# Decoder step with 64 experts: three experts at fixed places, second-layer weights in row pairs

## What is computed

```
x += MoE(RMSNorm(x))     # 64 sigmoid-routed experts, top 8 of 64 (in 4 of 8 groups), and 1 shared expert
expert e:  h = silu(xg @ w1[e]) * (xg @ w3[e]) * gate      # w1, w3: 1024 x 256
           y = h @ w2[e]                                    # w2: 256 x 1024
```

## Time and profile before

| | |
|---|---|
| time, median of 3 runs | 1083.21 us (1082.49 to 1084.88) |
| the profiled execution | 1083.57 us, span 1081.8 us |
| mean granted TensorE clock | 0.996 |
| PE busy | 1042.0 us, 96% of the span |
| DMA | 296.59 MB; 403 to 409 GB/s in most slices of the expert loop |
| DMA packets | 87203, of which 68453 under 8 KB |
| expert loop on TensorE | 365.2 us to 983.6 us |

### The profile page before, as it was taken

One profiled execution on the slowest core, in us unless ns is written; L12 is line 12 of the kernel. 1 busy time (PEld: TensorE's weight loads), 2 busy tenths in 40 slices (PEclk: granted clock), 3 DMA queues, 4 the chain that ended last, 5 costly groups with the idle time before them and its releaser, 6 DMA issues.

```text
span 1081.8 us, 11992 instructions
## 1 busy us (share of the span) xinstructions
PE 1042.0 (96%) x3692; PEld 513.9 (48%) x3692; DVE 454.0 (42%) x1286; ACT 166.4 (15%) x407; POOL 391.2 (36%) x459
## 2 busy tenths in 40 slices
PE   6999999899998999999999999999999989999996
PEld 4777555555544444444444444443444434443442
DVE  4200222345377634344343443443433343342884
ACT  3110023310120111111111111111110110112332
POOL 6000321200034544444454545454544453451231
PEclk9999999999999999999999999999999999999998
DMA  9032241320232999999999999999999998976931
GB/s 291 16 89 78 79 126 37 112 63 31 92 116 78 403 409 404 386 409 378 393 405 385 398 403 383 396 394 368 406 388 351 403 377 328 407 290 257 420 139 78
DMA packets 87203, 296.59 MB, mean 274 GB/s; under 512 B 18938, under 2 KB 29370, under 8 KB 68453
## 3 DMA queue, kind: packets, MB, share of 16 engines
q1 hardware_dynamic: 67885, 258.14, 62.4%
q0 software_dynamic: 19264, 37.82, 9.4%
HBM read 281.27 MB, written 36.73 MB: 294 GB/s over the span
## 4 chain that ended last, share of the span: by engine, by line
PE 83%; DVE 5%; DMA 5%; issue 3%; POOL 2%; ACT 1%; DVEq 1%; SPq 0%; POOLq 0%; ACTq 0%
PE bank L2218 27%; PE bank L1851 20%; PE bank L2200 15%; PE bank L2279 5%; PE bank L2215 5%; DMA arena<-xs_dram,slot 3%; PE bank L2197 2%; PE bank L1857 2%; DMA arena<-y_dram 1%; PE bank L2228 1%; PE bank L1937 1%; PE bank L1947 1%; POOL arena L878 1%; PE bank L1984 1%; PE bank L1846 1%
## 5 line engine op out<-in xcount | busy, mean ns | idle before, releaser
L878 POOL DMA_INDIRECT arena<-xs_dram,slot x232 | 244.1, 1052 | 79.9 <-issue 71.8
L2218 PE MATMUL bank<-arena 128*128 128x512 f32 x384 | 168.8, 592 | 0.0
L893 POOL DMA_INDIRECT y_dram<-arena,outrow x56 | 57.5, 1027 | 255.1 <-DVE slot L1660 230.6
L2200 PE MATMUL bank<-ring,arena 128*128 128x512 f32 x256 | 117.7, 603 | 0.0
L2218 PE MATMUL bank<-ring,arena 128*128 128x512 f32 x256 | 112.6, 593 | 1.2 <-DVE arena L1674 1.2
L1674 DVE STREAM_TRANSPOSE arena<-arena 128x1024 f32<-128x1024 f32 x58 | 72.2, 1245 | 98.9 <-DMA arena<-xs_dram,slot 98.9
L2218 PEld LDWEIGHTS bank<-arena 128*128 128x128 f32 x384 | 71.1, 190 | 80.4 <-issue 80.4
L1851 PE MATMUL bank<-xT,ring 128*128 128x288 f32 x384 | 93.4, 406 | 0.0
L1851 PEld LDWEIGHTS bank<-xT,ring 128*128 128x128 f32 x384 | 72.9, 190 | 20.5 <-issue 0.5
L1096 ACT ACTIVATE arena<-bank 128x256 f32<-128x256 f32 x56 | 21.6, 385 | 361.7 <-PE bank L2218 296.2
L2218 PEld LDWEIGHTS bank<-ring,arena 128*128 128x128 f32 x256 | 47.4, 190 | 55.6 <-issue 53.6
(11 more groups left out here) (391 smaller groups left out, 1216.4 us busy)
## 6 DMA issues: line engine op xcount, KB each, us to landing
arena<-in_ex_w SPq DMA_DIRECT2D x96, 1024.0 KB
ring<-in_ex_w SPq DMA_DIRECT2D x64, 1024.0 KB
mixpj<-in_ex_w SPq DMA_DIRECT2D x32, 1024.0 KB
arena<-y_dram SPq DMA_DIRECT2D x18, 1024.0 KB, 10.9
ring<-in_w_in SPq DMA_DIRECT2D x5, 2048.0 KB, 8.8
ring<-in_w_out SPq DMA_DIRECT2D x2, 2048.0 KB, 9.2
ring<-in_w_ple_gate SPq DMA_DIRECT2D x2, 2048.0 KB, 15.0
arena<-xs_dram,slot POOLq DMA_INDIRECT x232
```

Source lines behind the costliest of these rows:

```text
L878: pool.indirect_dma_start(xg[b][:, 256 * a:256 * a + 256], None, xs_quarter, bass.IndirectOffsetOnAxis(slot[k][:, a:a + 1], 0), bounds_che ...
L893: pool.indirect_dma_start(y_dram, bass.IndirectOffsetOnAxis(outrow[b][:, 0:1], 0), og[b], None, bounds_check=K * T - 1, oob_is_err=False). ...
L2200: ins = pe.matmul(bank[5 + half][:, :], hT[:, c, :], w2s[m % 4][:, c, n], start=(c == 0), stop=(c == 1))
L2218: ins = pe.matmul(bank[2][:, :], xgT[b][:, c, :], w13[m % 4][:, :, wc, :], start=(c == 0), stop=(c == KT - 1))
```

## The change

Experts 63, 62 and 61 get the first three steps whatever their counts: their `revs` are set to 3, 2 and 1 times 65536, which is more than any key of the others. For the other 61 experts the keys stay as they were. SP loads these three without waiting for `order`; the wait for `s_order` is moved behind the waits of L616 and L617. POOL's constants take one more iota and one multiplication, each tied to the one before. `load2` gives partition p the rows 2p and 2p+1 of w2, one piece of 8 KB, and to match, the two transposes take the even and the odd columns of `hh` instead of its halves.

```diff
+    FIXED = 3
...
             def load2(k, e):
-                sp.dma_start(w2s[k], ex_w2[0, bass.ds(e, 1)].rearrange("a (c p) n -> p (a c) n", p=P)
+                sp.dma_start(w2s[k], ex_w2[0, bass.ds(e, 1)].rearrange("a (p c) n -> p (a c) n", c=2)
                              ).then_inc(s_w2[k], 16)
...
-            sp.wait_ge(s_order, 2)
-            for m in range(3):
-                e = expert(m)
-                load13(m, e)
-                load2(m, e)
+            for m in range(FIXED):
+                load13(m, NE - 1 - m)
+                load2(m, NE - 1 - m)
             after(sp, "sh", NT - 1)
...
             after(sp, "y", NT - 1, 0)
             wait_drained(sp, "pT", NT - 1)
+            sp.wait_ge(s_order, 2)
             e = expert(3)
...
-            link(pool.iota(rev_i, pattern=[[-1, NE]], base=NE - 1, channel_multiplier=0))
+            pool.iota(rev_i[:, 0:NE - FIXED], pattern=[[-1, NE - FIXED]], base=NE - 1, channel_multiplier=0)
+            link(pool.iota(rev_i[:, NE - FIXED:NE], pattern=[[1, FIXED]], base=1, channel_multiplier=0))
             pool.tensor_copy(rank_row, rank_i)
             pool.tensor_copy(ids, id_i)
-            pool.tensor_copy(revs, rev_i).then_inc(s_const, 1)
+            link(pool.tensor_copy(revs, rev_i))
+            pool.tensor_scalar(revs[:, NE - FIXED:NE], revs[:, NE - FIXED:NE], float(1 << 16), None, ALU.mult
+                               ).then_inc(s_const, 1)
...
                     for c in range(2):
-                        ins = pe.transpose(bank[4][:, P * c:P * c + P], hh[:, P * c:P * c + P], ident[:, :])
+                        ins = pe.transpose(bank[4][:, P * c:P * c + P], hh[:, c:FF:2], ident[:, :])
```

## The result

The changed kernel takes 1086.87 us (median of 7, 1086.37 to 1088.19) against 1083.01 us for the kernel before on the same chip: ratio 1.0026, 95% interval 1.0015 to 1.0037. It is slower: by 3.9 us between the two medians, by 2.8 us (1.6 to 4.0) by the ratio. The forecast was 5.1 us less. The span of its profiled execution is 1084.8 us, 3.0 us longer than before. Lines of the changed kernel stand three lower for most of the code: its first matmuls are L2221 (L2218 for a pair), its picks L2144 and L2152, its transposes L2231, DVE's turning L1677 and product L1724, the gather L881.

The account below looks back on a forecast made before the run. TensorE was taken as the bound, DMA within a few per cent. Gaps 4.4 plus clock 1.7 less gathers 1.0 gave 5.1 us less than 1083.57: 1078.5 us profiled, 1078.1 us median; range for 8 in 10: 1074 to 1086 us.

Parts of the forecast that it names:

- Gathers beside bigger pieces: At PE's picks: gathers queue behind larger weight pieces, 0 to 2.1 us later; taken as 1.0 us lost in all.
- rival C: At the picks: turn-taking delays each gather 0.6 us, losing 6.2 us; 1089 us, or 1083 to 1084 with gaps shrunk; chance 0.17.
- point of decision: At the single steps: a loss once gathers land more than about 0.7 us later, for then these steps pay too.
- B: Whole kernel: nothing measurable, slow engines lag regardless of piece size, hole never on PE's path; 1082 to 1084 us; chance 0.22.
- The gaps: PE's waits for weights at pair steps of periods 5 to 7: 6.7 us shrink to 2.3 us.
- dip of the clock: PE's clock at 0.76 and 0.67 behind the longest gap, costing 1.7 us; expected to go.
- the early load and order: At the later gaps: the head start takes 1 us off, the order of experts adds 0.4 us.
- a few slow DMA engines: In the weight loads: some engines fall behind by some 2 us each period until pair steps show gaps.
- The strided turn: PE's transposes of even and odd columns: taken as no cost; at worst 60 ns a load, 6.7 us.
- the hole: DMA nearly idle at 1 GB/s between 320 and 345 us; the 9.4 MB of early weights move in it.
- the last long gap: PE's 3.51 us wait for weights at the period 7 pair step; no gap should stay that long.
- The marks named for a wrong prediction: New pick waits for DVE, DVE's gather waits over 2 us; transpose loads of 150 ns or more; or unchanged gaps, periods 5-7.

Follow-up runs that it names:

- before_swap: Kernel before, with the one-hot builds ahead of the turning of the gathered rows on DVE: 1084.90 us, ratio 1.0011.
- w2_turn_swap: Kernel before, with 8 KB w2 packets, even/odd turn and one-hot builds first, without fixed experts and early load: 1079.43 us, ratio 0.9959.

## Why the prediction was wrong

**The step that failed** is "Gathers beside bigger pieces": "I take 0.1 us at each of 8 pairs and at two or three tight single steps, 1.0 us in all." Its mechanism was the right one, and it stood there as rival C; the size of the term was off. The bound for the lateness, 0 to 2.1 us, held the measured 0.93 us. But the term took next to nothing of that bound and gave no ground for it. The measured price is 10.5 us: 6.0 at the pairs' picks and 4.5 elsewhere. The measured terms add up to the loop's 2.8 us: 8.5 less at the weights' gaps, 10.5 more behind the gathers, 0.8 more in the clean loop.

**Rival C** gave +0.6 us and 6.2 us of loss, and 1083 to 1084 us with the gaps shrunk. It had the pairs nearly right: 0.55 us of 0.6, where each of the 8 pairs paid (7.3 - 1.3) / 8 = 0.75 us of 0.93. It had the lateness too small and the single steps in the wrong places: 0.3 us at six tight ones, 1.8 us in all, where 4.5 us were paid, over half of it at the two turns of the loop's body, where DVE stands 5 us in any case. That its point of decision, 0.7 us, fits the result (0.93 us, a loss) is in part luck, for the single steps that it rests on are others. The ground given against C, that all gathers take about as long whatever is loading, could not carry it: in the kernel before they take from 4.4 to 7.4 us in the steps where DVE waited for them, and the loop has no stretch with other loads to compare with. In the chances, 0.22 for "same" is B's alone and leaves nothing for the part of C that is named with it.

**How full the DMA is.** The table ahead of the prediction has 403 to 409 GB/s in most slices of the loop. Eight of its 22 whole slices reach 403 GB/s; from 374 to 975 us the mean is 384 GB/s, at a DMA share of 0.98. The reading stands all the same: the engines are hardly ever free, so a gather has weight packets beside it.

**The gaps.** Forecast 4.4 us less waiting and no dip of the clock, 6.1 us together. Measured 8.5 us less, waits and clock together, but this is no measure of the packets alone: TensorE, held up by 12.2 us of other waits, gave the weights time. With the picks out of the way, before_swap to w2_turn_swap is 9.6 to 4.3 us, 5.3 for the packets against the 3.8 forecast, which were waiting alone; the early load and order then take it to 2.3 us, 2.0 against the 0.6 forecast (1.0 less 0.4). That a few slow DMA engines make these gaps was argued in the prediction, and no run here shows it or rules it out.

**The strided turn.** Taken at 0, with a bound of 60 ns a load. Measured 55 ns, near the upper bound, but 0.8 us in the clean loop in place of 6.7: the duration was wrong by all of it, the exposure saved most. A step of two floats costs a load most of what I had put at the far end.

The Trainium skill (SBUF — State Buffer, "Door 1: The DMA port swizzle") would have such a read at full rate, with two floats in each line of 16 bytes. By 196 ns against 141 ns in the same instruction that does not hold for these loads; the measurement decides.

**What was right.** SP's first load at 316 us, the hole at 375 GB/s, the first step unchanged (PE L2221 at 365.1 us), POOL's constants hidden, 8192 packets fewer, the last long gap and the clock dip gone. The marks named for a wrong prediction were the ones that appeared: pick waits for DVE, DVE's waits for gathers above 2 us, loads of over 150 ns.

## What to carry to other kernels

Packet size is a setting with two sides when a bulk queue and a queue of small, urgent transfers share the DMA engines: here 2 KB more of weight packet gave 5 us at the weights and cost 10 us at the gathers. Before making the bulk larger, find the work that stands behind the small transfers in program order without needing them, and move it ahead; the exchange of two calls turned a loss of 0.3% into a gain of 0.7%. And when a wait is removed from a loop that is near two bounds, ask which of them takes over: the same exchange gave nothing where the weights were still the bound.

## What the runs showed of the hardware that was not expected

- A packet of 4 KB takes a DMA engine 0.159 us and one of 8 KB for 0.311 us (medians in the loop), and behind a packet of rows an engine mostly turns to a weight packet (85% of the packets of 4 KB and more that follow, in the kernel before).
- Weight loads of 128 x 128 floats take 196 ns with a step of two floats and 141 ns with neighbouring ones.
- DVE's product of 128 x 256 floats takes 668 ns with its output at a stride of 128 floats and 484 ns with neighbouring ones.
- At both turns of the loop's body (ahead of the 29th and the 43rd step) DVE stood 4.3 to 5.8 us before its first instruction, in all 14 kernels. Each time an 8 KB packet of the instruction queue starts 2.0 to 2.2 us ahead of that instruction. At its entry into the body, ahead of the 15th step, DVE waited for ACT alone (2.31 us in the kernel before).
- Splitting 2 MiB of weights for each expert into packets of 4 KB in place of 8 cost 9.4 us at the weights' gaps (8.5 to 17.9), or 0.09 us a MiB over some 55 experts; the 1 MiB of w2, in 10 against 8, gives 5.3 us and 0.10 us. The two pure stretches had given 0.05 us, and the packets' own durations give 0.06 us a MiB (256 of 0.159 us against 128 of 0.311 us, on 16 engines). The figures from the gaps also hold what the clock lost behind a gap.
